# First modulation blocks taken in another order, first norm by halves, side loads reordered, column products in groups of eight

## The reference, cut to what matters

```python
s_lat = jax.nn.silu(c)
s_ctx = jax.nn.silu(c_ctx)
for l in range(DEPTH):
    mod = (s_lat @ ada_w[l] + ada_b[l])[:, None, :]
    sh1, sc1, g1, sh2, sc2, g2 = jnp.split(mod, 6, -1)
    modc = jnp.split(s_ctx @ ada_w[l][:, :n_mod * D_MODEL] + ada_b[l][:n_mod * D_MODEL], n_mod)
    a_lat = rms_norm(h, norm1_g[l]) * (1 + sc1) + sh1
    a_ctx = rms_norm(hc, norm1_g[l]) * (1 + modc[1]) + modc[0]
    if l % 2 == 0:
        y, yc = even_mixer(a_lat, a_ctx, ev_w_in[i], ...)
...
```

## Time and profile before

| | |
|---|---|
| median of 3 runs | 2882.91 us (2881.27 to 2885.45) |
| the profiled execution | 2877.25 us, of which the span is 2875.5 us |
| TensorE busy | 2717.3 us, 94% of the span |
| VectorE, ScalarE, GpSimd busy | 64%, 51%, 6% |
| mean granted TensorE clock | 0.965 of full |

### The profile page before, as it was taken

How to read it: one execution, slowest core, us unless ns; L and a number is a source line. 1 busy time by engine, 2 the same in 40 slices (tenths; PEclk the granted TensorE clock), 3 DMA queues, 4 the chain that set the end, 5 groups by cost and what they waited for, 6 DMA issues and landing times.

```text
span 2875.5 us, 34331 instructions
## 1 busy us (share of the span) xinstructions
PE 2717.3 (94%) x13129; PEld 2256.3 (78%) x13129; DVE 1850.9 (64%) x2339; ACT 1466.0 (51%) x2095; POOL 160.5 (6%) x206
## 2 busy tenths in 40 slices
PE   6999899999998979999999999998799999997998
PEld 5777678888885668888888788877678788787787
DVE  5676677687685555555888756479556555546555
ACT  5563354444462245445777545674355545553553
POOL 2111000000030000000000000002000000100100
PEclk9999899999997989999999999999899999999999
DMA  7773166676660045555999755550255555650444
GB/s 275 235 246 110 59 227 234 227 268 216 211 190 4 1 139 176 169 162 192 325 332 321 246 178 187 160 188 1 67 183 171 189 191 174 204 191 22 140 160 146
DMA packets 260641, 511.43 MB, mean 178 GB/s; under 512 B 9641, under 2 KB 40577, under 8 KB 260368
## 3 DMA queue, kind: packets, MB, share of 16 engines
q1 hardware_dynamic: 256576, 498.11, 51.6%
q0 software_dynamic: 3920, 11.36, 1.4%
HBM read 507.33 MB, written 1.05 MB: 177 GB/s over the span
## 4 chain that ended last, share of the span: by engine, by line
PE 86%; DVE 8%; ACT 3%; DMA 1%; issue 1%; POOL 1%; DVEq 0%; ACTq 0%; POOLq 0%; SPq 0%
PE bank L422 23%; PE bank L423 23%; PE bank L426 23%; PE bank L1351 2%; PE bank L1364 2%; DVE h_hid L2616 1%; DVE wlo L330 1%; PE bank L1377 1%; PE bank L393 1%; PE bank L394 1%; PE bank L395 1%; PE bank L2162 1%; PE bank L518 1%; ACT whi L326 1%; DMA raw<-in_moe_w 1%
## 5 line engine op out<-in xcount | busy, mean ns | idle before, releaser
L330 DVE TENSOR_TENSOR wlo<-raw,whi 128x1024 fp32r<-128x1024 f32 (+1 forms) x964 | 1140.6, 1198 | 716.4 <-ACT whi L326 710.2
L326 ACT ACTIVATE whi<-raw 128x1024 fp32r<-128x1024 f32 (+1 forms) x964 | 990.5, 1039 | 817.2 <-PE bank L426 775.2
L422 PE MATMUL bank<-whi,xhi 128*128 128x512 f32 (+2 forms) x2328 | 891.5, 383 | 22.8 <-DVE wlo L330 7.3
L426 PE MATMUL bank<-whi,xlo 128*128 128x512 f32 (+2 forms) x2328 | 883.3, 379 | 0.0
L423 PE MATMUL bank<-wlo,xhi 128*128 128x512 f32 (+2 forms) x2328 | 882.5, 379 | 0.0
L422 PEld LDWEIGHTS bank<-whi,xhi 128*128 128x128 f32 x2328 | 445.8, 191 | 104.9 <-issue 18.1
L426 PEld LDWEIGHTS bank<-whi,xlo 128*128 128x128 f32 x2328 | 444.7, 191 | 78.0
L423 PEld LDWEIGHTS bank<-wlo,xhi 128*128 128x128 f32 x2328 | 445.5, 191 | 75.6
L422 PE MATMUL bank<-whi,f_hhi 128*128 128x512 f32 x496 | 196.0, 395 | 0.0
L426 PE MATMUL bank<-whi,f_hlo 128*128 128x512 f32 x496 | 194.5, 392 | 0.0
L423 PE MATMUL bank<-wlo,f_hhi 128*128 128x512 f32 x496 | 192.7, 388 | 0.0
(11 more groups left out here) (545 smaller groups left out, 2884.1 us busy)
## 6 DMA issues: line engine op xcount, KB each, us to landing
raw<-in_ffn_w SPq DMA_DIRECT2D x180, 1024.0 KB, 5.2
raw<-in_moe_w SPq DMA_DIRECT2D x96, 1024.0 KB, 5.4
raw<-in_moe_w SPq DMA_DIRECT2D x48, 768.0 KB, 4.7
raw<-in_ada_w SPq DMA_DIRECT2D x24, 1024.0 KB, 5.3
raw<-in_ev_w_in SPq DMA_DIRECT2D x24, 1024.0 KB, 5.6
raw<-in_ffn_w SPq DMA_DIRECT2D x36, 512.0 KB, 3.6
raw<-in_hyb_w_in SPq DMA_DIRECT2D x18, 1024.0 KB, 5.1
raw<-in_attn_w_qkv SPq DMA_DIRECT2D x18, 1024.0 KB, 5.1
```

What stands on the lines that cost most here:

```text
L326: nc.scalar.activation(whole, part, ACT.Copy).then_inc(sem("w_hi"), 1)
L330: nc.vector.tensor_tensor(wlo[s][:, 0:rows, 0:n], part, whole.bitcast(F32), ALU.subtract)\
L422: nc.tensor.matmul(bank[:, 0:n], xk_h, whi[s][:, wk, 0:n], start=first, stop=False)
L426: ins = nc.tensor.matmul(bank[:, 0:n], xk_l, whi[s][:, wk, 0:n], start=False, stop=last)
```

## The change

1. `EARLY` becomes (0, 2, 1, 3): after two chunks the lower halves of shift and scale are there.
2. The column products of the first modulation are made in two lots of eight products, chunks 0 and 2 into `psum[3]` behind the second chunk, chunks 1 and 3 into `psum[4]` as a need of the first projection: TensorE first does the row blocks 0 and 1 of u8, then these products, then row blocks 2 and 3. VectorE takes them in two halves (`early_columns_dve`), each with four small operations.
3. The norm's transposes move from behind the second chunk to behind the third. ScalarE applies scale and shift in two halves of four (`first_norm_act`), VectorE cuts pairs 0 and 1 within the third chunk's turn and 2 and 3 behind the fourth's.
4. GpSimd's queue: x and the bias row go before the fourteen parameter loads, ctx goes behind the two roots of the first norm. TensorE's wait for the bias row moves behind the second chunk.
5. The 24 products of the second layer's columns become three groups of eight in each of the two stages: between the two U units of the fifth pair, behind the transposes in the sixth, and between the two U units of the sixth. VectorE takes the columns one step later. The order of the columns stays.
6. Regions are aligned to 128 bytes where it was 64, and `cT` (258 columns) moves behind `bias` and `gqk` in the region of the even mixer.

```diff
...
-            got[name] = inner.enter_context(nc.sbuf_tensor(f"{prefix}_{name}", shape, dt, align_bytes=64))
+            got[name] = inner.enter_context(nc.sbuf_tensor(f"{prefix}_{name}", shape, dt, align_bytes=128))
...
             self.s.unit(xhi, xlo, 0, 4, n, U, True, False)
+            if later:
+                later()
             self.s.unit(xhi, xlo, 4, 4, n, U, False, True)
...
             self.s.step(self.turned_lo(former, tile) if former else None)
-            self.s.step(also)
             self.s.step()
+            self.s.step(later)
             self.s.step(product)
...
-    def vector_columns_pe(e, st):
+    def vector_columns_pe(e, st, group):
 
         e.after(f"vec{st}:15")
-        at = 0
-        for p in ((0, 3), (1, 4))[st]:
-            for _, total in vec_sums(p):
-                for i in range(KD):
-                    ins = nc.tensor.matmul(O[1][:, at:at + 1], total[:, i * P:i * P + P], ones[:, 0:1], start=True, stop=True)
-                    at += 1
+        p, row = (st, 3 + st)[group // 2], group % 2
+        total = vec_sums(p)[row][1]
+        for i in range(KD):
+            at = KD * group + i
+            ins = nc.tensor.matmul(O[1][:, at:at + 1], total[:, i * P:i * P + P], ones[:, 0:1], start=True, stop=True)
         e.put(ins, f"vec cols_ps{st}")
...
-            f.pair(n, former, (lambda: vector_columns_pe(e, st)) if j == VEC_TURN else None)
+            turns = [lambda g=g: vector_columns_pe(e, st, g) for g in range(3)]
+            f.pair(n, former, turns[1] if j == VEC_TURN else None,
+                   turns[0] if j == VEC_TURN - 1 else turns[2] if j == VEC_TURN else None)
...
+        side_load(e, h[:, :, :], a["x"][0].rearrange("(t p) d -> p t d", p=P), "x")
+        e.link(nc.gpsimd.memset(mhalf[:, :], -0.5), "mhalf")
+        side_load(e, mr[4:5, :], a["ada_b"][0:1, 0:2 * D], "bias0")
         for tile, row, src in prm_src:
             side_load(e, params[row:row + src.shape[0], tile, :], src, "params")
-        for n, t in (("x", h), ("ctx", hc)):
-            side_load(e, t[:, :, :], a[n][0].rearrange("(t p) d -> p t d", p=P), n)
-        e.link(nc.gpsimd.memset(mhalf[:, :], -0.5), "mhalf")
         e.link(nc.gpsimd.memset(ones[:, :], 1.0), "ones")
...
-    EARLY = range(4)
+    EARLY = (0, 2, 1, 3)
...
     def late_pool(e, l, tag):
 
+        side_load(e, hc[:, :, :], a["ctx"][0].rearrange("(t p) d -> p t d", p=P), "ctx")
         e.after(f"{tag}:xT3")
...
+    EARLY_COLS = (psum[3], psum[4])
+
+    def mod_pe(e, s):
+
         e.after("spad")
-
-        e.eng.wait_ge(sem("y_done"), ffn.ys.n)
-        for c in EARLY:
+        for n, c in enumerate(EARLY):
             mod_chunk_pe(e, s)
-            if c == 0:
+            if n == 0:
                 params_pe(e)
-                loaded(e, f"bias{l}")
-            else:
-                e.eng.wait_ge(sem("out_done"), e.outs.n - 1)
-                column_products(psum[3], mr, (c - 1,))
-            if c == 1:
+            if n == 1:
+                e.eng.wait_ge(sem("out_done"), 2)
+                loaded(e, "bias0")
+                e.put(column_products(EARLY_COLS[0], mr, EARLY[0:2]), "mod0:cols0")
+            if n == 2:
                 e.after("params")
                 norm_pe(e, "in_e0")
-        e.eng.wait_ge(sem("out_done"), e.outs.n)
-        e.put(column_products(psum[3], mr, (3,)), f"mod{l}:cols")
+
+    def last_early_pe(e):
+
+        e.eng.wait_ge(sem("out_done"), 4)
+        e.put(column_products(EARLY_COLS[1], mr, EARLY[2:4]), "mod0:cols1")
+        e.after("in_e0:x1")
...
+    def mod_act(e, s):
+        for n, c in enumerate(EARLY):
             mod_chunk_act(e, s, c)
-            if c == 0:
+            if n == 0:
                 loaded(e, "x")
                 rms_act(e, h, "in_e0")
+            if n >= 2:
+                first_norm_act(e, n - 2)
+
+    def first_norm_act(e, half):
+
+        banks = norm_banks(e, "first")
+        scale, shift = modulated(0, 0, 0)
+        e.after(f"mod0:{half}")
+        for k in range(4 * half, 4 * half + 4):
+            e.after(f"in_e0:xT{k // 2}")
+            bank = banks[k // 2][:, (k % 2) * TOK:(k % 2) * TOK + TOK]
+            e.put(nc.scalar.activation(xf[:, k, :], bank, ACT.Identity, bias=shift(k), scale=scale(k)), f"in_e0:xf{k}")
...
+    def mod_dve(e, s):
+        for n, c in enumerate(EARLY):
             mod_chunk_dve(e, s)
-            if c == 0:
+            if n == 0:
                 params_dve(e)
-            elif c == 1:
+            elif n == 1:
                 norm_scaled_dve(e, h, "in_e0")
-        mod_columns_dve(e, 0, gain1(l), f"mod{l}:cols", f"mod{l}", psum[3])
+                early_columns_dve(e, 0)
+            elif n == 2:
+                cut_x(e, "in_e0", range(2), lambda b: f"in_e0:xf{2 * b + 1}")
+        early_columns_dve(e, 1)
+        cut_x(e, "in_e0", range(2, 4), lambda b: f"in_e0:xf{2 * b + 1}")
...
```

More of the change, by code:

```diff
@@ L209, in program @@
     R_E = region("e", p=([P, 2, NT, 6 * N], F32), qT=([P, 4, 2 * TOK], F32), kT=([P, 4, 2 * TOK], F32),
-                 cT=([P, 4, TOK + 2], F32), bias=([P, 2, NT, TOK], F32), gqk=([P, 2 * HD], F32))
+                 bias=([P, 2, NT, TOK], F32), gqk=([P, 2 * HD], F32), cT=([P, 4, TOK + 2], F32))
     OW = 2304
@@ L519, in turn_over, with pair @@
             ins.then_inc(sem("turned"), 1)
-        def pair(self, n, former, also=None):
+        def pair(self, n, former, also=None, later=None):
             self.eng.wait_ge(sem("silu_done"), self.pairs.at(0))
@@ L619, in turned_lo, with pair @@
             return work
-        def pair(self, n, former, tile, also=None, roots=None):
+        def pair(self, n, former, tile, later=None, roots=None):
             def product():
@@ L1172, in mod_load @@
             ld.columns(a["ada_w"][l], D, c * N, N)
-    def mod_pool(e, l, *deps):
-        e.after(*deps)
-        side_load(e, mr[4:5, :], a["ada_b"][l:l + 1, 0:2 * D], f"bias{l}")
     def late_pool(e, l, tag):
+        side_load(e, hc[:, :, :], a["ctx"][0].rearrange("(t p) d -> p t d", p=P), "ctx")
         e.after(f"{tag}:xT3")
-        if l:
-            e.after("res_f1:h")
         side_load(e, late_rows[4:5, :], a["ada_b"][l:l + 1, 3 * D:5 * D], f"late{l}")
@@ L1203, in mod_columns_pe @@
         e.put(column_products(psum[7], rows, range(4)), name)
-    def mod_pe(e, s, l, ffn):
+    EARLY_COLS = (psum[3], psum[4])
+    def mod_pe(e, s):
         e.after("spad")
-        e.eng.wait_ge(sem("y_done"), ffn.ys.n)
-        for c in EARLY:
+        for n, c in enumerate(EARLY):
             mod_chunk_pe(e, s)
-            if c == 0:
+            if n == 0:
                 params_pe(e)
-                loaded(e, f"bias{l}")
-            else:
-                e.eng.wait_ge(sem("out_done"), e.outs.n - 1)
-                column_products(psum[3], mr, (c - 1,))
-            if c == 1:
+            if n == 1:
[3 more added lines that the diff above has]
+            if n == 2:
                 e.after("params")
                 norm_pe(e, "in_e0")
-        e.eng.wait_ge(sem("out_done"), e.outs.n)
-        e.put(column_products(psum[3], mr, (3,)), f"mod{l}:cols")
+    def last_early_pe(e):
+        e.eng.wait_ge(sem("out_done"), 4)
+        e.put(column_products(EARLY_COLS[1], mr, EARLY[2:4]), "mod0:cols1")
+        e.after("in_e0:x1")
     def late_pe(e, s, l, st):
@@ L1266, in mod_columns_dve, with early_columns_dve @@
                                                   scalar=1.0, in1=gain, op0=ALU.add, op1=ALU.mult), name)
-    def mod_dve(e, s, l):
-        for c in EARLY:
+    def mod_dve(e, s):
+        for n, c in enumerate(EARLY):
             mod_chunk_dve(e, s)
-            if c == 0:
+            if n == 0:
                 params_dve(e)
-            elif c == 1:
+            elif n == 1:
                 norm_scaled_dve(e, h, "in_e0")
-        mod_columns_dve(e, 0, gain1(l), f"mod{l}:cols", f"mod{l}", psum[3])
+                early_columns_dve(e, 0)
[3 more added lines that the diff above has]
+        cut_x(e, "in_e0", range(2, 4), lambda b: f"in_e0:xf{2 * b + 1}")
+    def early_columns_dve(e, half):
+        e.after(f"mod0:cols{half}")
+        ks = slice(4 * half, 4 * half + 4)
+        got = EARLY_COLS[half][:, 0:32].rearrange("p (a k s) -> p a k s", a=2, s=2)
+        for i in range(2):
+            e.link(nc.vector.tensor_copy(mod[:, i, ks, :], got[:, i, ks, :]))
+        for st in range(2):
+            e.link(nc.vector.scalar_tensor_tensor(out=scal[:, 0, ks, st], in0=mod[:, 1, ks, st], scalar=1.0,
+                                                  in1=gain1(0)[:, ks], op0=ALU.add, op1=ALU.mult), f"mod0:{half}")
     def cut_pair(e, name, b, of=None):
@@ L3238, in _ @@
             setup_pool(e)
-            mod_pool(e, 0)
             norm_pool(e, "in_e0")
@@ L3285, in _ @@
             s.first()
-            mod_act(e, s, 0)
+            mod_act(e, s)
             for st in range(2):
-                if st == 0:
```

(8 more changed lines are left out.)

## The result

The changed kernel takes 2858.62 us, the median of 4 runs (2856.62 to 2860.24), where the kernel before had 2884.18 (4 runs, 2881.27 to 2889.0). The ratio is 0.9916, 95% interval 0.9901 to 0.993: 24 us faster, between 20 and 29. The changed kernel was timed once more, against the kernel before on the same chip, as e6: there the ratio was 0.9932 (0.9919 to 0.9945), 19.6 us. The forecast was 12.9 us less and 2870.0, with a range from 2861 to 2879.

The account below looks back on a forecast made before the run. TensorE, busy 94% of the span, was taken as the bound, so gains come from its waits or lower clock. Start 7.6, groups 5.3 and alignment 0 sum to 12.9 us: 2882.9 to 2870.0, range 2861 to 2879.

Parts of the forecast that it names:

- The start, 7.6 us: Up to the first projection block's end: new order and side loads move it from 63.45 to 55.8, bounds 3 and 11.
- 43 as a sign of being wrong: At the start: the fourth chunk's copy, forecast at 42.2 to 42.8, coming later than 43 would count against the prediction.
- The premise under it: Start, before 35.12: 2.76 us idling, 1.05 of small products and 1.7 of transposes left matmuls 0.23 apart, clock not lowered.
- Sum 5.3: Second layer's column products, two stages: groups hold the clock, 6.3 us gained less 1.0 for joints; bounds 0 and 6.3.
- I take 0, bounds 1 us either way: Region tiles at new addresses: alignment changes nothing, since matmuls reading region and base tiles take 395 and 397 ns.
- my slower rival: Feed-forward matmuls on region tiles: new layout slows them, 6 ns each costing 13.3 us and cancelling all; 5 in 100.
- Units too late: Start: weight units come late, so it gains only 3 us, total about 8 or 3, 2875 to 2880; 13 in 100.
- Groups that do not hold the clock: Second layer's column products: the clock still falls once a stage, gain 7.6 - 1.0, 2876.3 us; 12 in 100.
- fall three times: Second layer's column products: each group costs the clock, 9.4 us against 7.6, giving 2884 to 2886; 4 in 100.
- Layout, slower: Feed-forward matmuls: from 9 ns more each (19.9 us, 2890) the kernel is slower by over 0.2%; 5 in 100.
- More than forecast: Whole kernel: start and groups at their upper bounds and the layout too, 2862 us or less; 7 in 100.

Follow-up runs that it names:

- e11: The changed kernel with the first eight column products behind the third chunk in place of the second; 2859.87 us, ratio 0.9922 to the kernel before.
- e12: The changed kernel with the first eight products behind the third chunk and ctx asked for only behind the norm's transposes; 2856.64 us, ratio 0.9915.
- run 16: Not the name of a run: "run" is a verb here, and 16 counts the products and the transposes that e11 and e12 execute.
- e2: The kernel before with only the second layer's column products split into three groups of eight; 2870.4 us, ratio 0.996.
- e5: The kernel before, unchanged, timed again as if new, giving a second trace; 2882.87 us, ratio 1.0009 to the kernel before.
- e10: The changed kernel with the first two groups of eight products joined behind the sixth pair's transposes, the third alone; 2866.15 us, ratio 0.9944.

## Why the prediction was off, step by step

- **The start, 7.6 us: right.** Against the mean of six old traces (64.6) it is 7.5; against the one trace that I had, 6.5. The steps were right too: the fallen clock in the third chunk, no wait for parameters, a DMA stream that does not bind. Missed: the clock falls already in the wait ahead of the small products (3.5 us for 2.0) and stays down until 36.1, so the projection starts 1.1 us later than forecast. The fourth copy is at 43.22 where I had 42.8 and had named 43 as a sign of being wrong.
- **The premise under it, that the clock stands after 2.76 us of idling and transposes: a single trace.** In five of six traces of the old start the clock fell there; that I had the one in which it stood was luck. On the strength of its 0.23 at 35.12 I set aside the Trainium skill's rule that transposes do not count as busy (page "TensorE: Matmul & The Clock Gate", section "PE-mode transpose"). The other traces do not decide on that rule: four of the five falls come ahead of any transpose, and e11 and e12 run 16 products and 16 transposes, 3.6 us, without a fall. The premise cost the forecast 1.2 us only, the distance of the lucky trace from the mean.
- **The column groups, "Sum 5.3" with the bound 6.3: this step failed, in size.** e2 measures 11.5 (7.8 to 15.6). The joints cost 0.1 us each and not 0.25. The second stage loses 4.2 and not 2.7 in six of the seven traces with the one lot. And there are short falls of the clock, some 1.5 us each, which I had not counted: near 582 us (five of the seven) and near 780 (four of seven), both some 80 us behind a lot; in none of the seven traces with groups of any cut. The one near 582 follows 1.98 us of four gate products (L1066). Of the second kind the first trace had one, at 779.0, which I overlooked. Matched matmul by matmul, e2 gains on e5 3.1 us in the first stage, 1.6 near 582, 4.7 in the second stage and 1.3 near 780: 10.7. Why a lot far ahead should make the short falls likelier is open.
- **Alignment, "I take 0, bounds 1 us either way": this step failed.** The object of my slower rival was right and its sign wrong: the old place was the bad one. 4.6 us by the distances, 1.4 to 8.9 timed. The row that I read, 395 against 397 ns, compares overlapping lengths, and `xhi`'s mean includes every start after a wait and every stretch at the lower clock. The distance between two starts, which I used everywhere else, shows 231.3 against 227.1 ns in the trace that I had.
- **The whole.** 7.5, 10.7 and 4.6 make 22.8, between the 24.2 and 19.6 measured. My upper bounds, 11, 6.3 and 1, make 18.3, less than either. The profiled execution of before, 2877.25, was the quickest of its five; a forecast made against it is low in what the clock can give back.
- **The rivals.** Units too late: no (e12). Groups that do not hold the clock, or fall three times: no. Layout, slower: no, it was faster. More than forecast: yes, at 7 in 100 too cheap.

## What to carry to other kernels

Keep runs of one-column or two-column matmuls short and put full matmuls between them: 16 instructions (1.7 us) between full matmuls left the clock alone, and 32 of one column (3.5 us) cost 2.7 us in each place of e10. This is no law of a count: 16 products and 16 transposes (3.6 us) in e11 and e12 cost nothing, and 2.94 us of waiting cost the clock at the start. Let large stationary tiles begin at a multiple of 128 bytes, for here 64 past cost 2 ns a matmul in the mean and 32 past 5 to 6. To price a layout, compare distances of starts in stretches without waits, and take where the clock falls from several traces, not from one.

## What the runs showed of the hardware

- Behind a matmul of 128 x 512 whose stationary tile begins 64 bytes past a multiple of 128 (by the sizes in the code), the next one starts 229.4 to 231.3 ns later with `whi` as the moving side, 226.2 with `wlo`; at 32 past 233.0 to 233.5 with either; at 0 227.0 to 227.1. Why 64 past costs nothing behind `wlo` I did not test.
- The same kernel at the same place, 8 us with 2.75 us of idling and 16 transposes, had a granted clock of 1.00 in one execution and 0.57 in another. 16 transposes take 1.94 us at the one level and 3.65 at the other.
- While x, on GpSimd's queue, and the weights, on SyncE's, were both under way, u1 was cut from 12.86 on, where it had been cut from 11.7 on before: the estimate of 12.8 for its landing held.
